# Second block's step list rewritten, first block's reordered, filler products dropped, norm factor applied at the read of the up panels

## What is computed

```python
# first block
h = rms_norm(x, mix_norm_g)
proj = h @ w_in                                  # 1024 -> 3*256 + 3*256 + 1024 + 2*256 + 4*1024
merged = sum(gates[b] * (branch[b] @ out[b]) for b in range(4))  # conv, stick-breaking, RWKV-7, spatial gating
x = x + merged @ w_o
h = rms_norm(x, ffn_norm_g)
up = causal_dwconv(h @ w_up, conv_w)             # three taps over positions, 2 * 2816 columns
gate, val = split(up, 2)
x = x + (silu(gate) * val) @ w_down
x = rms_norm(x, final_norm_g)
# two layers
for l in range(2):
    proj = rmsnorm(h, norm_mix[l]) @ w_in[l]     # 768 columns main, 256 columns queries to the memory
    if l == 0:
        main_out = pool_mixer(main)              # means over 2, 4, 8, 16 positions, then pool_w
    else:
        k, v = rmsnorm(h, kv_norm) @ w_kv        # 4 heads of 64; k normed per head
        main_out = window_attention(rmsnorm(q), k, v, sinks)   # 12 heads, window 128, slope * distance
    mk, mv = rmsnorm(mem, mem_norm[l]) @ w_mem_kv[l]
    mem_out = softmax(rmsnorm(mq) @ rmsnorm(mk).T / 8) @ mv    # 4 heads
    h = h + concatenate([main_out, mem_out]) @ w_out[l]
    h = h + square(relu(rmsnorm(h, norm_mlp[l]) @ w_up[l])) @ w_down[l]
```

## Time and profile before

| what | us |
|---|---|
| median of 3 runs | 1126.67 |
| lowest, highest | 1126.12, 1137.84 |
| the profiled execution | 1134.23 |
| its span in the trace | 1132.4 |
| DVE busy, ACT busy, POOL busy | 711.1, 549.3, 95.2 |
| `wlo` on DVE, 156 operations | 360.4 |
| `whi` on ACT, 156 operations | 295.5 |

### The profile page before, as it was taken

How to read it: one execution, slowest core, us unless ns; L and a number is a source line. 1 busy time by engine, 2 the same in 40 slices (tenths; PEclk the granted TensorE clock), 3 DMA queues, 4 the chain that set the end, 5 groups by cost and what they waited for, 6 DMA issues and landing times.

```text
span 1132.4 us, 20562 instructions
## 1 busy us (share of the span) xinstructions
PE 1069.4 (94%) x8570; PEld 1004.8 (89%) x8570; DVE 711.1 (63%) x857; ACT 549.3 (49%) x709; POOL 95.2 (8%) x64
## 2 busy tenths in 40 slices
PE   4998999899898899999989999999999889999998
PEld 3987789899788899999877999999998579999998
DVE  5677445644667777777884555555689836545453
ACT  4546345352544555656543553434475544544442
POOL 0050021100020000000253200000020002000000
PEclk9999899999999999999999999999999889999999
DMA  6534233234362555455323455464543114554551
GB/s 239 200 136 149 75 112 112 78 111 149 107 212 76 181 192 203 169 213 177 96 73 112 149 187 205 168 204 168 205 165 113 38 42 146 203 206 168 203 174 50
DMA packets 24804, 168.77 MB, mean 149 GB/s; under 512 B 2753, under 2 KB 3137, under 8 KB 5154
## 3 DMA queue, kind: packets, MB, share of 16 engines
q1 hardware_dynamic: 23616, 164.64, 41.7%
q10 hardware_dynamic: 1122, 3.17, 0.9%
HBM read 166.75 MB, written 1.05 MB: 148 GB/s over the span
## 4 chain that ended last, share of the span: by engine, by line
PE 72%; DVE 15%; ACT 7%; issue 3%; POOL 2%; DMA 1%; SPq 0%; ACTq 0%; DVEq 0%; POOLq 0%
PE G L544 11%; PE G L545 11%; PE G L546 11%; PE D L544 8%; PE D L546 8%; PE D L545 8%; DVE wlo L1556 4%; ACT whi L1108 2%; PE M L545 2%; PE M L546 2%; PE M L544 2%; PE D L740 1%; DVE cv L1900 1%; PE M L726 1%; PE M L744 1%
## 5 line engine op out<-in xcount | busy, mean ns | idle before, releaser
L1556 DVE TENSOR_TENSOR wlo<-raw,whi 128x2048 fp32r<-128x2048 f32 (+1 forms) x156 | 360.4, 2314 | 150.3 <-ACT whi L1108 150.2
L544 PE MATMUL G<-xh,whi 128*128 128x256 f32 (+1 forms) x1264 | 362.3, 287 | 11.7 <-DVE xl L1578 5.5
L545 PE MATMUL G<-xl,whi 128*128 128x256 f32 (+1 forms) x1264 | 353.8, 280 | 0.0
L546 PE MATMUL G<-xh,wlo 128*128 128x256 f32 (+1 forms) x1264 | 353.6, 280 | 0.0
L1108 ACT ACTIVATE whi<-raw 128x2048 fp32r<-128x2048 f32 (+1 forms) x156 | 295.5, 1897 | 80.6 <-PE D L546 80.2
L544 PEld LDWEIGHTS G<-xh,whi 128*128 128x128 f32 (+1 forms) x1264 | 238.8, 189 | 20.9 <-issue 8.3
L545 PEld LDWEIGHTS G<-xl,whi 128*128 128x128 f32 (+1 forms) x1264 | 238.3, 189 | 1.8 <-issue 1.5
L546 PEld LDWEIGHTS G<-xh,wlo 128*128 128x128 f32 (+1 forms) x1264 | 237.6, 188 | 0.0
L544 PE MATMUL D<-hh,whi 128*128 128x256 f32 x688 | 193.1, 281 | 2.8 <-DVE wlo L1556 1.7
L545 PE MATMUL D<-hl,whi 128*128 128x256 f32 x688 | 192.7, 280 | 0.0
L546 PE MATMUL D<-hh,wlo 128*128 128x256 f32 x688 | 192.7, 280 | 0.0
(11 more groups left out here) (370 smaller groups left out, 1556.0 us busy)
## 6 DMA issues: line engine op xcount, KB each, us to landing
raw<-wall_dram SPq DMA_DIRECT2D x152, 1024.0 KB, 4.9
raw<-wnarrow_dram SPq DMA_DIRECT2D x4, 768.0 KB, 4.3
x<-x_dram SPq DMA_DIRECT2D x4, 256.0 KB, 5.5
mem<-mem_dram ACTq DMA_DIRECT2D x1, 1024.0 KB, 5.0
out_dram<-x SPq DMA_DIRECT2D x4, 256.0 KB, 2.5
poolw<-pool_w_dram ACTq DMA_DIRECT2D x1, 576.0 KB, 6.9
cst<-cst_dram ACTq DMA_DIRECT2D x1, 416.0 KB, 9.1
lora<-lora_dram ACTq DMA_DIRECT2D x1, 256.0 KB, 6.2
```

The lines of the kernel that those rows point to most:

```text
L544: mm(out, w_h, hi, start=start, stop=False, skip_group_check=skip)
L545: mm(out, w_h, lo, start=False, stop=False, skip_group_check=skip)
L546: return mm(out, w_l, hi, start=False, stop=stop, skip_group_check=skip)
L1556: signal(tt(wlo[:, pan.slot, 0:w], raw[:, pan.slot, 0:w], f32(whi[:, pan.slot, 0:w]), SUB), "w_lo")
```

## The change

1. Every `warm` goes but the four products of `warm_start`.
2. The norm before the first FFN is done like the later ones: `part(1, i)` splits `x * gain` into `mh` and `ml` behind each `wo` panel, and DVE applies the root as it reads an up panel into `upad`. The root is computed behind the first up panel. All three FFNs read `mh`/`ml`, the memory's products and `kv` read `xh`/`xl`; the memory's scaling and split move into late iterations of the FFN before (`LATE`).
3. `add_squares` leaves four tiles of squares and not one, so every statistic is four products. A Newton step is three operations, not four.
4. In the second block most panels are cut into halves and a step of an attention stands between the halves. `wout0` and `wout1` are laid out by pair of inputs (`out_pair`): panels 0 and 1 need one pair each, panel 2 two, and the four results lie in G0, G1, M0, M1.
5. Queries aren't normed any more. Products of the squares with two columns of ones give sums per position (`sums_of`, 128 x 2), and the factor goes into `exp`'s scale or into the addition of the distance term. Gains of queries and keys are multiplied into the keys.
6. Probabilities aren't scaled before they are turned: `turn_p` and `turn_s` multiply them (f32 products) by a diagonal matrix of the reciprocals, `dgm` or `dg`, that DVE writes in one operation per attention or group.
7. In the first block `rw_key` is cut in three (`rw_square`, `rw_key`, `rw_scale`), `sg_mean` comes before `sc`, table loads of ACT before the waits, splits in `out` panels behind the branch's steps (`ahead_lo`); the last three slots, not one, are kept free of RWKV steps; `sg_mix` adds its bias on DVE.

The weights' order in DRAM follows. Here is the diff of the lists and of the functions named (a line of "..." is left out).

```diff
-RW_ENDS = 1
+RW_ENDS = 3
...
-          ("panel", PAN["sb"]), ("sg_gelu",), ("panel", PAN["sb"] + 1), ("rw_turn",), ("sc",),
-          ("panel", PAN["sb"] + 2), ("sg_mean",)]
+          ("panel", PAN["sb"]), ("sg_gelu",), ("panel", PAN["sb"] + 1), ("rw_turn",),
+          ("panel", PAN["sb"] + 2), ("sg_mean",), ("sc",), ("ahead_lo", PAN["sb"] + 2)]
...
-    W += [("mem_load",), ("panel", PAN["wo"]), ("panel", PAN["wo"] + 1), ("mem_squares",)]
-    W += [("panel", PAN["wo"] + 2), ("mem_stat",), ("panel", PAN["wo"] + 3)]
-    W += [("norm", 1), ("mem_norm", 0), ("ffn", 0), ("squares", 2)]
+    W += [("mem_load",), ("panel", PAN["wo"]), ("part", 1, 0), ("panel", PAN["wo"] + 1), ("mem_squares",), ("part", 1, 1)]
+    W += [("panel", PAN["wo"] + 2), ("mem_stat",), ("part", 1, 2), ("panel", PAN["wo"] + 3), ("part", 1, 3)]
+    W += [("sums", 1), ("ffn", 0), ("squares", 2), ("sums", 2)]
...
+    m0, q1, k1, q2 = PAN["in0m"], PAN["in1"], PAN["kv"], PAN["in1b"]
+    o0, o1 = PAN["wout0"], PAN["wout1"]
...
+          ("turn_mv", 0), ("square_m", 0), ("panel", m0), ("sum_m", 0), ("ahead", m0 + 1), ("begin", m0 + 1), ("score_m", 0), ("panel", m0 + 1), ("exp_m", 0), ("pool", 3),
+          ("soft_m", 0), ("panel", m0 + 2), ("pool", 2), ("begin", m0 + 3), ("turn_p", 0), ("panel", m0 + 3),
...
+    W += [("pool_mm", 3), ("ahead", o0), ("begin", o0), ("pool_mm", 2), ("panel", o0),
...
+          ("begin", q2), ("ahead", q2), ("turn_p", 1), ("panel", q2), ("square_s", 1), ("turn_v",), ("score_s", 0),
+          ("begin", q2 + 1), ("ahead", q2 + 1), ("sum_s", 1), ("pv_m", 1), ("exp_s", 0), ("root_s", 1), ("panel", q2 + 1),
+          ("soft_s", 0), ("out_m", 1), ("square_s", 2), ("score_s", 1), ("turn_s", 0), ("sum_s", 2), ("pv_s", 0), ("out_s", 0)]
+    W += [("begin", o1), ("exp_s", 1), ("root_s", 2), ("soft_s", 1), ("score_s", 2), ("ahead", o1), ("panel", o1),
...
             if n == 0:
                 warm_start()
-            elif n == 1:
-                warm(19, "D0")
...
         def turn_p(l):
...
-            if l == 0:
-                warm(36, "M0")
...
-                        ins = nc.tensor.transpose(DB[h][:, mt, tt * P:(tt + 1) * P],
-                                                  pm[:, 2 * h + tt, mt * P:(mt + 1) * P], ident)
...
+                        ins = mm(out[:, mt, tt * P:(tt + 1) * P], pm[:, 2 * h + tt, mt * P:(mt + 1) * P],
+                                 dgm[:, 2 * h + tt, :])
...
+        def sums_of(out, sem):
+
+            for b in range(2):
+                for j in range(2):
+                    ins = mm(out[:, 4 * b + 2 * j:4 * b + 2 * j + 2], hsq[:, j, b * P:(b + 1) * P], two)
...
                     if nu == 2:
                         t = 2 * j + u
+                        if js == 0 and u == 0:
+                            more(pan, 2)
+                            own(nc.vector.memset(upad[:, :, :, 0:2], 0.0))
+                            root(FNORM[f])
+                        dve.wait_ge(S("pe_panel"), pan.p + 1)
+                        signal(tt(upad[:, u, :, 2:T + 2], G[u][:, :, :], rstd[:].unsqueeze(1).broadcast_to([P, 2, T]), MUL),
+                               f"up_read{f}")
```

More of the change, by code:

```diff
@@ L1113, in split_to @@
                 done[0] += 1
-        NORM_AFTER = {"wout0": 4, "wout1": 6}
         def squares(n):
-            for i in range(3 if n in NORM_AFTER.values() else 0, 4):
+            for i in range(4):
                 square(n, i)
```

873 lines of the change are left out of this document (527 added, 346 removed).

## The result

The changed kernel took 1074.87 us (median of 4 runs, 1074.38 to 1075.03), the kernel before 1129.54 beside it (4 runs, 1126.12 to 1137.84): a ratio of 0.9505 with a 95% interval of 0.9448 to 0.9562, so faster by 5%. (Some executions of any of these kernels are slower by a per cent or more; the ratios leave those out, the medians and ranges don't, so a ratio isn't the quotient of its two medians.) From profiled execution to profiled execution it is 1134.23 to 1074.38 us, -59.9, where the forecast's sum was -60. The sum is right to the microsecond and several of its terms are not; most of what follows is about that.

The account below looks back on a forecast made before the run. TensorE was taken as the bound, with 86 us lost to idle and filler. Terms summed to -60: 1074 on the profiled 1134.2, 1067 on the median 1126.7; 1068 was taken, own range 1052 to 1083, full range 1046 to 1096.

Parts of the forecast that it names:

- Branches, -22: First block up to the first `wo` panel: reordering, fillers gone, bias off PE and clock given back save 22 us (10 to 28).
- `wo` to FFN, -12: `wo` and the first FFN's start: unnormalised first panel and later root save 12 us (7 to 14).
- Nothing waits: At the first FFN panel: the last operand link takes about 3 us while pairs 0 to 2 give PE 4.1.
- The first FFN, +1 (0 to +6): First FFN's loop: the memory's scaling and split in two late iterations can make a split late, +1 us (0 to +6).
- Memory attention, -17: Memory attention and pooling: half-panels and alternated steps cover waits, small products cost +3, clock gives -2; together -17 us (-8 to -20).
- Windowed attention, -13: Windowed attention up to `wout1`: cover -18.3, small products +8.8, clock -3.5; together -13 us (-3 to -19).
- the first (thin cover, clock down): Outside the FFNs, chains end later and PE waits without filler: gain only 31 to 40 us, 1087 to 1096; chance 0.18.
- The second: DVE bounds the first FFN: at 18 us an iteration, nine lose 15 us, giving 1083 us; chance 0.07.
- fourth: Whole kernel slower: TensorE at 1.2 GHz where fillers had held it, losing the 60 us and 11 more; chance 0.03.
- fifth: Panels in the gaps need late operands, so waits only move and time stays within 1%; chance 0.03.
- The third: More than forecast: both later FFNs at 0.113 and no halved clock before 900, 1050 us or below; chance 0.09.
- the rule that I weighed against the change: Long idle gaps between bursts of products lower the clock, so fillers taken out without cover would cost twice.

Follow-up runs that it names:

- the two kernels above: Changed kernel with the RWKV branch's last additions straight behind `rw_gn2` again, 1074.9 us; changed kernel with the first block's step order put back at four places, 1078.4 us.
- a_dfree: Changed kernel with TensorE asking for banks D0 to D3 at an FFN's first down product, not ahead of its first up panel: 1070.3 us.
- a_root1: Changed kernel with norm 1's statistic ahead of FFN 0's first panel, TensorE waiting there until DVE begins the Newton step: 1074.6 us.
- a_tail: Changed kernel with a_dfree's edit, and late weight splits and the memory's split put behind the last `hid` of FFN 0: 1063.6 us.
- b_nofill: Kernel before with its 174 filler products left out, the four at the start kept, order unchanged: 1137.8 us against 1133.8, ratio 1.0043.
- a_rwend: Changed kernel with the RWKV branch dealt over all slots but the last, its last additions straight behind `rw_gn2`: 1074.9 us.

## Why the prediction came out right, and where it was wrong

The direction and the size were right: 1074.87 in a range of 1046 to 1096, 7 above the 1068 taken, and that difference is the choice of base (the sum was right on the profiled execution; the median fell 54.7 from 1129.54). By its own terms:

1. **Branches, -22 against -27.8.** Idle and filler went from 26.1 to 10.5 us, where I left 10.8: right. Summed from start to start over the traces, the 1,536 weight products took 189.6 us before and 184.8 after, -4.8 where the clock's term had -3.5 (28 of them ran at half clock before, none after), and the small products 73.6 and 66.2, -7.4 where the term had -2.9. So most of the miss is the small products. Here is PE's timeline at `sg_mix`, before: first and last of the 16 products that alternate between the mixing (L830) and the bias (L831), then the next weight product; and after it the same place of the changed kernel.

```profile
118.29 0.43 PE L830 MATMUL D<-sgw,sgn 128*64 128x128 f32 x2
...
124.12 0.69 PE L831 MATMUL D<-sgb,cst 1*64 1x128 f32 x2
...
127.80 0.58 PE L544 MATMUL G<-xh,whi 128*128 128x256 f32 x1
```

```profile
111.06 1.09 PE L905 MATMUL D<-sgw,sgn 128*64 128x128 f32 x16
112.09 0.66 PE L914 MATMUL D<-cst,z_sb 128*128 128x128 f32 x4
...
113.74 0.38 PE L586 MATMUL G<-xh,whi 128*128 128x256 f32 x1
```

`sg_mix` took 6.45 us and takes 1.03. A product of one row alternating with one of 128 gave one start in 0.36 us, and from 123 on less, since the granted clock went to half with PE busy throughout (0.76 from 121.3 to 124.8, 0.50 behind); the small products behind it took 3.06 us, now 1.65, and the first weight products were at half clock too. In all 6.8 us against my 2.9, for which I had taken a row of 3.9 us of busy time that counts L831's records alone. This is read from two traces; the bias was not put back by itself. The other edits of this stretch weren't tried singly either, but for the two kernels above.

2. **`wo` to FFN, -12 against -8.9.** "Nothing waits" was the step that failed. I followed the operands and not the banks: `ffn` waits for D0 to D3 as well, 3.0 us and 2.7 at half clock. The 2.5 us left for the unnamed nearly held the wait (3.1 of idle in all); the half clock behind it had no term here, and that is the miss. a_dfree takes the half clock away and leaves 0.8 us of wait, for `ml`, so the operands were late too, by a little. The late root did what was said (a_root1: about 4.9 us).

3. **The first FFN, +1 (0 to +6) against +10.4.** DVE, the feared bound, was none. Seven iterations of DVE:

```profile
352.68:471.40 118.72, 100.53 (x143) 1.00 0.55 191
```

   100.5 us over seven is 14.4 an iteration (forecast under 15.5), and PE is idle for none of it (118.72 us busy). The loss came where I had not looked, at the end of the loop: I had written that a split might be late and priced it with up to 6 us for the memory's two operations in the middle, where nothing is late. At the end it is 4.7 of wait, where before had 1.0, and 1.7 of half clock (a_tail), and 5.1 of pace, which stands in the prediction as something unexplained and in no term of its sum: 10.5 in all.

4. **Memory attention, -17 against -14.7.** Idle 4.6 (4 left), small products +2.9 (+3). The clock gave back less than the 2 forecast: weight products 64.7 to 63.5.

5. **Windowed attention, -13 against -21.2.** Two terms. "I leave 6": 2.4 stayed. And +8.8 of small products with -3.5 of clock make +5.3, where small products measured -0.6 (starts added up, 35.3 to 34.7) and weight products +1.5 (68.2 to 69.8, none of them at half clock in either kernel). The new ones cost about what I took.

   A turn takes 0.225 us from start to start (0.26 forecast, 52 of them), a sum 0.22 (0.2). What I had wrong is the base: in the earlier trace rows's stretch, the third window, the old small products ran at half clock. The 36 transposes of the windowed softmax took 6.8 us there, 0.19 each and not the 0.12 of the earlier trace rows. I priced the new products at full clock and the old ones as if they had it too, and gave the clock a lump that was too small.

6. **FFN 2 and 3, +3 against +2.3.** Right.

The errors (-5.8, +3.1, +9.4, +2.3, -8.2, -0.7) add to nothing but rounding: the sum's accuracy was luck, and the range was what carried the forecast. Of the rivals, the first (thin cover, clock down) came true at two places, for 7.7 us of wait and 4.4 of half clock. The second, fourth and fifth didn't come. The third neither: both later FFNs stayed at the slower pace. A gap inside the first FFN, which I had said would prove me wrong, is there at its end. Of the rule that I weighed against the change, b_nofill gives the size: 76 us of gaps without filler put 183 weight products at half clock, not 43, and some 13 us on them, not as much again as the gaps.

How the -59.9 divides over the parts of the change is known only where a run takes a part out: `wout1`'s place 12.6, the late root 4.9, the halves of panels 2.9, the order at the start about 3.5. Most of the branches' and of memory attention's gain is read from stretches and wasn't tried singly.

## To carry to other kernels

Follow every wait of an instruction, the accumulator banks' too, and not only its operands: what is asked for early is waited for early. Look at both ends of a loop that you shift work into, not only at its middle. Fillers cost what they overrun, and taken out alone they brought nothing; a useful panel in their place did (12.6 us for two panels of `wout1`). Price old work at the clock it ran at, not the clock that it should have.

## What was not expected of the hardware

- The pace of weight products (128x256, same instructions, granted clock 1.00) has two values, 0.113 and 0.1175 us. Inside the FFNs it changed only where PE was interrupted, by a wait or by small products, and otherwise held, for up to 1,536 products; at `out3` it changed with no interruption. It is worth 5 to 7 us an FFN. It differs between executions of one kernel: shown for the first panels of the changed kernel and the control (108 against 104 records in 12 us), likely for whole FFNs (the runs of a_rwend spread over 10.8 us).
- A single wait of 3.0 or 4.7 us inside dense products is followed by 5.4 and 3.4 us at 1.2 GHz.
- Sixteen f32 products that alternate between 128 rows and one (L830, L831) took 6.45 us, the eight of 128 rows alone 1.03; and the granted clock fell to half during them although PE had not been idle since 112.2 us, 11 us earlier.
